# The lower parts of the weights computed on GpSimd instead of VectorE, in a one-core kernel for a hybrid attention and recurrent layer

## The reference

```python
xn = rmsnorm(x, g_in)
h = xn @ w_in                                   # 1024 x 5648
dq, dk, dv, dg, gq, gk, gv, gg, ga, mg = split(h)
oa = softmax(q1 k1) v - lam * softmax(q2 k2) v  # 4 heads, block-causal
ob = gated_linear_attention(gq, gk, gv, log_sigmoid(ga @ w_alpha_up + b_alpha) / 16)
oa = rmsnorm(oa) * (1 - lam_init) * silu(dg)
ob = rmsnorm(ob) * silu(gg)
mixed = sigmoid(mgA) * (oa @ w_branch_a) + sigmoid(mgB) * (ob @ w_branch_b)
y = rmsnorm(x + mixed @ w_out)
```

## Time and profile before

| | |
|---|---|
| median of three runs | 1034.79 us |
| profiled execution, span | 1033.86 us, 1032.1 us |
| DVE busy | 483.9 us (47%), 1107 instructions |
| ACT busy | 329.2 us (32%), 775 instructions |
| POOL busy | 44.5 us (4%), 77 instructions |
| DMA | 75.51 MB, 73 GB/s on average |
| chain that ended last | PE 83%, DVE 10%, ACT 4%, issue 3%, DMA 1% |

### The profile page before, as it was taken

One profiled execution on the slowest core, in us unless ns is written; L12 is line 12 of the kernel. 1 busy time (PEld: TensorE's weight loads), 2 busy tenths in 40 slices (PEclk: granted clock), 3 DMA queues, 4 the chain that ended last, 5 costly groups with the idle time before them and its releaser, 6 DMA issues.

```text
span 1032.1 us, 15277 instructions
## 1 busy us (share of the span) xinstructions
PE 960.8 (93%) x6204; PEld 884.0 (86%) x6204; DVE 483.9 (47%) x1107; ACT 329.2 (32%) x775; POOL 44.5 (4%) x77
## 2 busy tenths in 40 slices
PE   5989999999999979999899989998899799979997
PEld 4979998989998868998789878997898699978884
DVE  6531276642047654255445634553356656562222
ACT  5452322222222322235424432343334422130010
POOL 1000000010000000000000000000000000000000
PEclk9989999999999999999999999999899899989999
DMA  9011111131111021510312030301222363432221
GB/s 307 11 38 46 37 43 42 60 94 42 41 48 29 2 63 53 187 47 1 83 42 85 10 84 16 98 21 29 55 73 95 126 208 125 150 120 72 92 84 70
DMA packets 86168, 75.51 MB, mean 73 GB/s; under 512 B 3682, under 2 KB 77811, under 8 KB 85971
## 3 DMA queue, kind: packets, MB, share of 16 engines
q1 hardware_dynamic: 86098, 74.54, 23.3%
HBM read 54.81 MB, written 19.73 MB: 72 GB/s over the span
## 4 chain that ended last, share of the span: by engine, by line
PE 83%; DVE 10%; ACT 4%; issue 3%; DMA 1%; POOL 0%; SPq 0%; POOLq 0%; ACTq 0%; DVEq 0%
PE proj_bank L1287 16%; PE proj_bank L1289 16%; PE proj_bank L1288 16%; PE score_banks L1287 6%; PE score_banks L1288 6%; PE score_banks L1289 6%; PE out_bank L1500 4%; PE score_banks L1468 3%; PE score_banks L1411 2%; DVE gla_scores L1125 2%; PE transpose_bank L1485 2%; PE transpose_bank L1373 1%; DVE level_scores L1118 1%; PE transpose_bank L1431 1%; DVE branches_lo L1160 1%
## 5 line engine op out<-in xcount | busy, mean ns | idle before, releaser
L1287 PE MATMUL proj_bank<-x_hi,w_hi 128*128 128x352 f32 x1080 | 360.1, 333 | 0.5 <-DVE w_lo L557 0.5
L1289 PE MATMUL proj_bank<-x_hi,w_lo 128*128 128x352 f32 x1080 | 350.6, 325 | 0.0
L1288 PE MATMUL proj_bank<-x_lo,w_hi 128*128 128x352 f32 x1080 | 350.5, 325 | 0.0
L1287 PEld LDWEIGHTS proj_bank<-x_hi,w_hi 128*128 128x128 f32 x1080 | 206.9, 192 | 2.6 <-issue 2.0
L1288 PEld LDWEIGHTS proj_bank<-x_lo,w_hi 128*128 128x128 f32 x1080 | 206.9, 192 | 0.0
L1289 PEld LDWEIGHTS proj_bank<-x_hi,w_lo 128*128 128x128 f32 x1080 | 206.0, 191 | 0.0
L557 DVE TENSOR_TENSOR w_lo<-w_raw,w_hi 128x1024 fp32r<-128x1024 f32 x53 | 64.8, 1223 | 98.0 <-ACT w_hi L553 97.8
L905 ACT ACTIVATE probs<-score_banks,softmax_stats 128x128 f32<-128x128 f32 (+8 forms) x72 | 51.2, 713 | 73.8 <-DVE softmax_stats L1179 62.2
L1220 DVE SCALAR_TENSOR_TENSOR branch_out<-out_bank,branch_norm_gains,da_gate 128x128 f32<-128x128 f32 (+1 forms) x36 | 12.2, 338 | 115.3 <-PE out_bank L1508 115.3
L1287 PE MATMUL score_banks<-w_out_hi,mixed_hi 128*128 128x512 f32 (+2 forms) x160 | 61.0, 381 | 5.6 <-DVE w_out_lo L557 5.6
L1287 PE MATMUL score_banks<-branches_hi,w_hi 128*128 128x352 f32 x192 | 64.1, 334 | 2.1 <-DVE branches_lo L1160 2.1
(11 more groups left out here) (159 smaller groups left out, 1221.9 us busy)
## 6 DMA issues: line engine op xcount, KB each, us to landing
w_raw<-in_w_in SPq DMA_DIRECT2D x45, 512.0 KB, 4.4
merge_tanh_scratch<-feature_stage SPq DMA_DIRECT2D x16, 528.0 KB, 3.1
feature_stage<-merge_tanh_scratch SPq DMA_DIRECT2D x8, 528.0 KB, 4.4
merge_tanh<-merge_tanh_scratch SPq DMA_DIRECT2D x8, 528.0 KB, 4.1
x_rows<-in_x_prompt SPq DMA_DIRECT2D x8, 512.0 KB, 7.7
branch_out<-in_x_prompt SPq DMA_DIRECT2D x8, 512.0 KB, 3.6
out<-branch_out SPq DMA_DIRECT2D x8, 512.0 KB, 2.6
gla_branch_scratch<-branch_out SPq DMA_DIRECT2D x1, 2112.0 KB, 8.4
```

Of the source, the lines that this page charges most:

```text
L1287: nc.tensor.matmul(out, wh, xh, start=first, stop=False)
L1288: nc.tensor.matmul(out, wh, xl, start=False, stop=False)
L1289: return nc.tensor.matmul(out, wl, xh, start=False, stop=last)
```

## The change

`split_lo` is issued on POOL in place of DVE, all 61 of them, with the same wait for ACT's rounded copy and the same semaphore behind it. DVE loses these instructions and their waits. POOL's list is put in the order of the stages: the powers of x are no longer nine in a row ahead of all else, but stand where `ms` stands, with the first subtractions between them; those of the branches after the list and of `w_out` follow, ahead of the powers of the output rows.

```diff
         def split_lo(w):
-            dve_.wait_ge(s_whi, w + 1)
-            nc.vector.tensor_tensor(halves(w)[1], raw_slot(w), halves(w)[0].bitcast(F),
+            pool_.wait_ge(s_whi, w + 1)
+            nc.gpsimd.tensor_tensor(halves(w)[1], raw_slot(w), halves(w)[0].bitcast(F),
                                     ALU.subtract).then_inc(s_wlo, 1)
...
-            for i in range(NTT):
-                pool.wait_ge(s_xms, i + 1)
...
             for st in stages:
-                if st[0] == "gO":
+                if st[0] == "ms":
+                    i = st[1]
+                    pool.wait_ge(s_xms, i + 1)
+                    n = ntok(i)
+                    nc.gpsimd.tensor_tensor(stat[0:n, 32 + i % 2:33 + i % 2], stat[0:n, 16 + i % 2:17 + i % 2], eps_pow[0:n, 0:1],
+                                            ALU.pow).then_inc(s_xrs, 1)
+                elif st[0] == "split":
+                    split_lo(st[1])
+                elif st[0] == "gO":
...
+            for f in range(1, KD_ - 1):
+                split_lo(NP_ + f + 1)
+            for w in range(NM, NW):
+                split_lo(w)
...
-                elif kind == "split":
-                    split_lo(st[1])
...
             for f in range(KD_):
-                if 1 <= f < KD_ - 1:
-                    split_lo(NP_ + f + 1)
...
             mixed_lo(3 * KD_ - 1)
-            for w in range(NM, NW):
-                split_lo(w)
```

More of the change, by code:

```diff
@@ L567, in second @@
             return ap.rearrange("p (b two w) -> p b two w", two=2, w=half)[:, 0:n // (2 * half), 1, :]
-        act_, dve_ = nc.scalar, nc.vector
+        act_, pool_ = nc.scalar, nc.gpsimd
         mg_last = FT[ft_no[ft_at["mg", 14]] % NFT]
@@ L952, in _ @@
             pool.wait_ge(s_half, 1)
-            for i in range(NTT):
-                pool.wait_ge(s_xms, i + 1)
-                n = ntok(i)
-                nc.gpsimd.tensor_tensor(stat[0:n, 32 + i % 2:33 + i % 2], stat[0:n, 16 + i % 2:17 + i % 2], eps_pow[0:n, 0:1],
-                                        ALU.pow).then_inc(s_xrs, 1)
             n_g = n_a = 0
             for st in stages:
-                if st[0] == "gO":
+                if st[0] == "ms":
[7 more added lines that the diff above has]
+                elif st[0] == "gO":
                     n = ntok(st[2])
```

## The result

The changed kernel takes 1046.40 us (median of four runs, 1043.34 to 1049.57) against 1033.93 us for the kernel before (four runs, three of them the ones above; 1030.97 to 1035.62): a ratio of 1.0121, with a 95% interval of 1.0096 to 1.0146. It is slower, by 12.5 us. Its profiled execution took 1046.62 us, 12.8 us over the one of before, so the two traces can be compared row by row.

A forecast was written before the change was run, and what follows sets the result against it. PE was taken as the bound, busy 960.8 of 1032.1 us. 4.6 + 3.8 + 1.0 = +9.4 us on 1033.86 us gave 1043.3, plus 0.9 for the median 1044.2 us; range 1039.3 to 1050.8 us.

The forecast's parts named there:

- One subtraction: Cost of one lower-part subtraction on POOL: taken as 2.3 us, with ends of 1.9 and 2.8 us.
- Part 1: Stage of `w_out`: its eight subtractions on POOL pace PE's four pieces, +4.6 us.
- Part 2: Recurrent branch: POOL's subtraction stops DVE's additions ahead of `k_to_end` for its full length, at two places, +3.8 us.
- The clock: PE's clock behind the new waits of 2.3, 0.7 and 1.6 us: taken to cost nothing, nothing added.
- Part 3: Small effects at the start, in the attention and at `branches_lo`: +1.0 us together.
- (a): Start: PE's first unit waits for the first lower part, between -0.4 and +1.1 us, taken as +0.3 us.
- (b): Attention: DVE's combination of the softmaxes is stopped by POOL, +0.4 us, and 0 without the stop.
- (c): Copy at 809.58 us: POOL runs until about 813.3 while `branches_lo` starts at 813.14, +0.3 us, up to +0.8.
- POOL yields: Rival: DVE is never stopped by POOL's subtractions; +3.9 us, 1038.7 us, chance 0.18.
- Slow POOL: Rival: a subtraction on POOL takes 4.6 us; +45 us, 1080 us, chance 0.11.
- fast POOL: Rival: a subtraction on POOL takes 1.7 us or less; -1.5 to +2.5 us, chance 0.08.
- Freed DVE: Rival: the time freed on DVE would by itself win over 3 us; chance 0.03.

The follow-up runs named there:

- e1: Changed kernel with the eight subtractions of `w_out` back on DVE, the other 53 on POOL; 1040.47 us, ratio to before 1.0050.
- e3: Changed kernel with 13 extra, never read matmuls on PE ahead of its wait for `k_to_end` at 212 and 404 us; 1044.41 us, ratio to before 1.0096.
- e2: Changed kernel with the subtractions of tiles 12 and 23 held on POOL until DVE has made `k_to_end`; 1038.46 us, ratio to before 1.0043.
- e4: Changed kernel with the changes of e1 and e2, and the border's subtraction moved behind `branches_lo`; 1033.77 us, ratio to before 0.9998.
- e7: Changed kernel with the subtractions of tiles 12 and 23 each done as eight pieces of 128 columns; one run, 1040.05 us.
- e5: Changed kernel with POOL copying the raw tile in place of each of the 61 subtractions, low-part corrections left out; one run, 1034.03 us.
- e6: Changed kernel with a POOL memset of the low part in place of each of the 61 subtractions, same corrections left out; one run, 1033.0 us.

## Why the prediction was right, and where it was off

The prediction said slower, +9.4 us, 1044.2 us; it is +12.5 us, 1046.40, inside the range of 1039.3 to 1050.8. The stops, the pace of `w_out` and, but for the border, their places were right; one step failed, and the range was wide enough to hold what it left out.

- **One subtraction**, 2.3 us: it is 2.33 to 2.42 where it runs undisturbed (the mean of 2.46 has eight in it that DVE held up in its turn, the longest 3.31 us). The sum of two reads and one write at 0.87 ns was not the reason, though: a copy (one read, one write) takes 1.04 us and a memset (one write) 0.95, so the write costs nothing beside one read, and the second read more than doubles the time. The middle of my bounds was lucky.
- **Part 1**, +4.6: measured +5.0. PE's wait of 7.9 us came as said; the two further waits are 1.52 and 1.55 us in place of 0.7 and 1.6. The first of them is longer because PE was back at full clock from 936 us, 4 us behind its start in place of the 6 that I had taken over from before, and so was done with its second piece sooner. That costs nothing, since POOL sets the end. `e1` shows that POOL's pace is the cause.
- **Part 2**, +3.8 for the stops: the stop is total, as taken, and costs 1.6 and 1.7 us net, +3.3 (`e3`), against 1.9 each. The stop itself was right (PE waits 2.26 and 2.12 us); what DVE's freed subtraction gives back was too small at 0.41, since `e2`, without the stop, is 0.7 and 0.4 us under before. But the places cost 3.1 and 3.3 us.
- **The clock**, "so I add nothing": this is the step that failed, by 3.0 us (1.5 at each place). The runs showed a granted clock of 0.58 to 0.60 behind each wait of 2.1 to 2.3 us, and `e3` that the clock is what costs. I argued from a wait of 2.67 us at 502 us that kept 1.00, to all waits of that length. The same wait is no safe reference: in `e2` it is as long, 2.66 us, and the clock is 0.50 behind it, 0.49 in place of 0.32 us for a product of 352 columns. Timeline of PE, `e2`, then before:

```profile
502.72 0.37 PE L1376 MATMUL transpose_bank<-ident,feature_stage 128*32 128x128 f32 x1 [2.66 <-ACT probsT L919]
...
503.18 0.49 PE L1291 MATMUL proj_bank<-x_lo,w_hi 128*128 128x352 f32 x1
```

```profile
502.97 0.32 PE L1288 MATMUL proj_bank<-x_lo,w_hi 128*128 128x352 f32 x1
```

- **Part 3**, +1.0: (a) 0.2 for 0.3, which isn't shown: in the other kernels with the same start (`e1` to `e4`, `e7`) the copy at 209 us is 0.2 to 2.8 us behind before; (b) 0.30 for 0.4, at the place named; (c) 0.6 for 0.3, by a stop of `da_out_normed`, which I had left out since it has one tile as its input. In sum 1.1.
- **The sum**: 0.2 + 6.4 + 0.3 + 0.6 + 5.0 = 12.5, with some 0.3 of small shifts and rounding 12.7, against 9.4. Of the 3.3 us between, 3.0 are the clock, 0.4 `w_out`, 0.1 part 3 and 0.3 small shifts, less 0.5 by the stops.
- **The rivals**: POOL yields is out by the 4.49 us. Slow POOL is out by 2.4 us. The fast POOL is what `e5` and `e6` make, and they land 0.3 and 1.3 us under their run of before, in the -1.5 to +2.5 us given for it. Freed DVE was to win over 3 us; `e2` shows 1.1 us at its two places, and `e4` in all no gain beyond its interval of 2 us.

## What to carry to other kernels

Before work is moved from DVE to GpSimd, ask of each place what DVE does while it runs: an instruction that reads SBUF there stops DVE's additions of two SBUF tiles for its whole length, and DVE's scaling of one SBUF tile was stopped even by a memset, while instructions that take one of their tiles from PSUM ran through. A stop costs where DVE is in PE's chain and nothing 3 us later. Order it behind that chain, or cut it into pieces as short as DVE's own instructions. And price a new wait of 2 us on PE with the clock too, 1.5 us here; behind the waits of 0.6 to 0.9 us in `e5` and `e7` the clock stayed at 1.00.

## What the hardware showed beside

- Whether PE's clock falls behind a wait of 2.7 us is not fixed by the work at the place. The wait at 502 us is 2.66 or 2.67 us long in all nine traces. 500 to 515 us has a granted clock of 1.00 in four of them (before, the changed kernel, `e1`, `e7`) and a mean of 0.89 in five (`e2` to `e6`). In 740 to 757 us it is the other way round for some: 0.90 in before, 1.00 in `e2`, `e4` and `e6`. 17 us at 0.90 are 1.7 us lost. A few such episodes, each there or not, are as large as the spread of the runs of one kernel (before: 1030.97 to 1035.62 us); that they are its cause wasn't tried. It is why the parts above are read from copy to copy at the place and not from medians. The border shows it too: `e2` has the same stop of `da_out_normed`, and yet the stretch took 28.60 us, less than the 28.94 of before, with the clock at 1.00 in 823.5 to 828.5 us where before has 0.66 in 825 to 830 us. In the changed kernel (832 to 837 us) and in `e4` (825 to 830 us) the clock is 0.66 as in before, so the 0.97 us between these two can be put down to the stop.
- A DVE instruction with one tile as input (`da_out_normed`, 128x128, scaled by two columns) is stopped as well, 2.37 us in place of 0.35, and by a memset too (`e6`), which the additions are not. So there are two kinds of stop here; which of DVE's other one-tile instructions belong to the second, no run here tells, since no other of that kind, from SBUF to SBUF and wider than two columns, started beside POOL's work.
